# HGRN values of the 16 leading tokens: eight fp32 products in four column strips, from raw weights, for heads 2 to 7

## The reference, cut to what matters

```python
def hgrn2_mixer(q, f_pre, i_in, g, lb, norm_g):      # proj = h @ w_in_c; q, f_pre, i_in, g = split(proj, 4)
    f = lb + (1.0 - lb) * jax.nn.sigmoid(f_pre)
    log_f, k = jnp.log(f), 1.0 - f
    ...                                              # chunks of 64 tokens; the first holds 48 of padding and the 16 meta tokens
    def step(state, xs):
        qc, kc, vc, lc = xs
        b = jnp.cumsum(lc, axis=2)
        b_last = b[:, :, -1:, :]
        ...                                          # scores and the chunk's output
        state = exp(b_last)[..., None] * state + einsum('bhsd,bhse->bhde', kc * exp(b_last - b), vc)
```

## Time and profile before

| | |
|---|---|
| median of 3 runs | 1340.23 us (1338.8 to 1343.05) |
| the profiled execution | 1339.83 us |
| its span | 1337.8 us |
| granted TensorE clock, mean | 0.989 |
| PE / PEld busy | 1291.7 us (97%) / 1178.7 us (88%) |
| DVE / ACT / POOL busy | 815.8 us (61%) / 631.7 us (47%) / 323.0 us (24%) |

### The profile page before, as it was taken

The page is one execution under the profiler, slowest core; times in us unless marked ns, Lnnn a source line. Parts: engine busy times, 40 slices in busy tenths (PEclk is TensorE's granted clock), DMA queues, the critical chain, the costliest instruction groups (busy, mean ns, idle before and its releaser), DMA issues.

```text
span 1337.8 us, 23152 instructions
## 1 busy us (share of the span) xinstructions
PE 1291.7 (97%) x9766; PEld 1178.7 (88%) x9766; DVE 815.8 (61%) x1360; ACT 631.7 (47%) x982; POOL 323.0 (24%) x179
## 2 busy tenths in 40 slices
PE   7999998999999999999999999999999999999996
PEld 6999855989999999999998988877787898998984
DVE  6999654456657276384656456465557673745745
ACT  5243487445446345253465335265353462552724
POOL 0001154355110201102654124114652102011040
PEclk9999999999999999999999999999999999999997
DMA  6221100222222223223222222212212333232311
GB/s 192 89 65 33 65 1 1 68 91 64 96 95 95 95 95 99 92 95 106 84 64 64 64 64 64 64 63 95 95 64 95 95 102 100 95 114 95 106 52 63
DMA packets 109031, 108.35 MB, mean 81 GB/s; under 512 B 8096, under 2 KB 106608, under 8 KB 108928
## 3 DMA queue, kind: packets, MB, share of 16 engines
q1 hardware_dynamic: 108528, 106.77, 24.8%
q10 hardware_dynamic: 400, 0.11, 0.0%
HBM read 104.77 MB, written 2.10 MB: 80 GB/s over the span
## 4 chain that ended last, share of the span: by engine, by line
PE 80%; DVE 10%; ACT 6%; issue 2%; POOL 0%; DMA 0%; DVEq 0%; SPq 0%; ACTq 0%
PE pb L808 41%; PE pb L1014 6%; PE pb L1016 6%; PE pb L1015 6%; PE pb L977 2%; PE pb L978 2%; PE pb L979 2%; PE pb L820 1%; PE pb L1251 1%; PE pb L917 1%; PE pb L918 1%; PE pb L855 1%; PE pb L916 1%; DVE wl L2124 1%; ACT wh L1467 1%
## 5 line engine op out<-in xcount | busy, mean ns | idle before, releaser
L670 POOL TENSOR_TENSOR wl<-raw,wh 128x2048 fp32r<-128x2048 f32 x40 | 185.3, 4633 | 685.9 <-ACT wh L1467 685.9
L808 PE MATMUL pb<-hidh,wh 128*128 128x264 f32 (+1 forms) x744 | 197.9, 320 | 0.2 <-DVE wl L2124 0.2
L808 PE MATMUL pb<-hidl,wh 128*128 128x264 f32 (+1 forms) x744 | 197.5, 320 | 0.0
L808 PE MATMUL pb<-hidh,wl 128*128 128x264 f32 (+1 forms) x744 | 197.4, 320 | 0.0
L1467 ACT ACTIVATE wh<-raw 128x2048 fp32r<-128x2048 f32 x73 | 139.3, 1908 | 88.3 <-DMA raw<-in_mlp_w_down 61.0
L808 PE MATMUL pb<-hh,wh 128*128 128x264 f32 (+1 forms) x584 | 150.0, 318 | 5.0 <-DVE qd L2766 1.6
L808 PE MATMUL pb<-hh,wl 128*128 128x264 f32 (+1 forms) x584 | 145.0, 309 | 0.0
L808 PE MATMUL pb<-hl,wh 128*128 128x264 f32 (+1 forms) x584 | 144.9, 309 | 0.0
L808 PEld LDWEIGHTS pb<-hidh,wh 128*128 128x128 f32 x744 | 123.7, 188 | 10.4 <-DVE wl L2124 0.7
L808 PEld LDWEIGHTS pb<-hidh,wl 128*128 128x128 f32 x744 | 123.4, 188 | 9.7
L808 PEld LDWEIGHTS pb<-hidl,wh 128*128 128x128 f32 x744 | 123.4, 188 | 9.4
(11 more groups left out here) (472 smaller groups left out, 3260.0 us busy)
## 6 DMA issues: line engine op xcount, KB each, us to landing
raw<-in_mlp_w_up SPq DMA_DIRECT2D x32, 1024.0 KB, 5.3
raw<-in_mlp_w_down SPq DMA_DIRECT2D x32, 1024.0 KB, 5.1
raw<-in_w_in_c SPq DMA_DIRECT2D x16, 1024.0 KB, 5.3
raw<-in_w_in_ab SPq DMA_DIRECT2D x8, 1024.0 KB, 6.0
raw<-in_w_out_ab SPq DMA_DIRECT2D x4, 1024.0 KB, 5.0
raw<-in_w_out_c SPq DMA_DIRECT2D x4, 1024.0 KB, 5.1
x_tok<-in_x SPq DMA_DIRECT2D x2, 1024.0 KB, 8.0
raw<-in_s_w_glu SPq DMA_DIRECT2D x1, 1024.0 KB, 5.4
```

The source lines that it names most:

```text
L670: pool.tensor_tensor(wl[:, c % RING, :], raw[:, c % RING, :], wh[:, c % RING, :].bitcast(F32), ALU.subtract).then_inc(w_lo, 1)
L808: mm = pe.matmul(pb[:, bank + b, 0:z_ - a], lhs, rhs[:, a:z_], start=first and hi and k == 0, stop=last and k == len(todo) - 1)
```

## The change

- For p = 1 to 3 the tile of the 16 leading tokens is left out of `run_tok`. In its place `lead_values(p)` issues eight fp32 products, one for each block kc of 128 input features: 32 columns of `h` as weights (16 leading tokens and 16 others), the raw weights of the slot, 256 columns, streamed. Product kc writes to the 32 partitions from 32 (kc mod 4), so that four follow each other in four column strips of PE, and the second four are added to the first four.
- The result is not summed over the strips: each of the four groups of 32 partitions holds a part of the values. ACT copies all 128 partitions to `v1[:, 0]`. The sum over the strips comes with the product in `chunk_sums`, since the keys are laid out four times: DVE writes them to columns 0 to 15, 32 to 47, 64 to 79 and 96 to 111 of a margin of 112 in front of `kd`, zero elsewhere. The keys are turned with 112 columns instead of 16, and the product contracts over 112 rows (16 for heads 0 and 1).
- `lead_values(p)` stands in q's tile 0 after the second step (n = 1), and waits for the slot's transfer only. It uses the odd bank beside q's tile 0, which was free already.
- It reads `raw`. So POOL's low half of i{p}, which overwrites it, now also waits for `v16_done`.
- The tile k = 1 of i{p} is now the first, and still waits for q's tile 1 to be taken; k = 2 waits for q's tile 0.
- One `memset` of the margin on DVE, before layer 1.

```diff
+V16 = [STAGES[f"i{p}"][0] for p in range(1, NPAIR)]
...
+        kd_home = sb("kd", [P, 8, LEAD + L], F32, m1k)
+        kd, ke0 = kd_home[:, :, LEAD:], kd_home[:, :, 0:LEAD]
...
+            return 2 * (STAGES[f"q{p}"][2] % 2) + 1      # v16_bank(p)
...
                     pool.wait_ge(w_hi, rank(c) + 1)
+                    if c in V16:
+                        pool.wait_ge(v16_done, V16.index(c) + 1)
                     pool.tensor_tensor(wl[:, c % RING, :], raw[:, c % RING, :],
...
                     for k, (a, rows) in enumerate(starts):
+                        if c in V16 and k == 0:
+                            continue
...
+                        elif c in V16 and k == 2:
+                            pe.wait_ge(*emptied(f"q{name[1]}", 0))
...
-                pe.transpose(pb[0:16, 6, 0:P], ke[:, i % 4, 0:16], ident[:, :])
+                pe.transpose(pb[0:LEAD, 6, 0:P], ke0[:, i, :], ident[:, :])
...
-                pe.matmul(pb[:, 4, 0:P], kdt[0:16, 0, :], v1[0:16, 0, vc], start=True, stop=True, skip_group_check=True)
+                rows = 16 if i < 2 else LEAD
+                pe.matmul(pb[:, 4, 0:P], kdt[0:rows, 0, :], v1[0:rows, 0, vc], start=True, stop=True, skip_group_check=True)
...
+            def lead_values(p):
+                c = V16[p - 1]
+                pe.wait_ge(w_in[c % RING], 16 * (c // RING + 1))
+                for kc in range(KC):
+                    j = 32 * (kc % 4)
+                    mm = pe.matmul(pb[j:j + 32, v16_bank(p), 0:256], h[:, kc, 0:32], raw[:, c % RING, kc * 256:(kc + 1) * 256],
+                                   start=kc < 4, stop=kc >= 4, skip_group_check=True)
+                mm.then_inc(v16_done, 1)
...
                 def in_q(t, n):
+                    if p and t == 0 and n == 1:
+                        lead_values(p)
                     if p and t == 0 and n == 3:
                         mean_squares(a)
...
+                if p and k == 0:                          # take_v(p, k), on ACT
+                    act.wait_ge(v16_done, p)
+                    act.activation(v1[:, 0, p * 256:(p + 1) * 256], pb[:, v16_bank(p), 0:256], ACT.Copy).then_inc(emptied_by["act"], 1)
+                    return
...
+            me.step(dve.memset(ke0[:, :, :], 0.0))
...
-                TT(ke[:, n % 4, 0:NMETA], kd[:, n, 0:NMETA], elast[:, n, 0:1].broadcast_to([P, NMETA]),
-                   ALU.mult).then_inc(f_ke, 1)
+                TT(kd_home[:, n, 0:P].rearrange("p (j c) -> p j c", j=4)[:, :, 0:NMETA],
+                   kd[:, n, 0:NMETA].unsqueeze(1).broadcast_to([P, 4, NMETA]),
+                   elast[:, n, 0:1].unsqueeze(2).broadcast_to([P, 4, NMETA]), ALU.mult).then_inc(f_ke, 1)
```

More of the change, by code:

```diff
@@ L272, in trunk @@
         m1k = ExitStack()
-        kd = sb("kd", [P, 8, LEAD + L], F32, m1k)[:, :, LEAD:]
+        kd_home = sb("kd", [P, 8, LEAD + L], F32, m1k)
+        kd, ke0 = kd_home[:, :, LEAD:], kd_home[:, :, 0:LEAD]
         qd = sb("qd", [P, 8, LEAD + L], F32, m1k)[:, :, LEAD:]
@@ L481, in trunk @@
         g_prod = sem("g_prod")
+        v16_done = sem("v16_done")
         k_turned = sem("k_turned")
@@ L567, in free_bank, with v16_bank @@
             return emptied_by[by], n
+        def v16_bank(p):
+            return 2 * (STAGES[f"q{p}"][2] % 2) + 1
         def out_bank(t, half):
@@ L979, in run_tok @@
                             mm = pe.matmul(o, hl[:, kc, a:a + rows], wh[:, c % RING, w], start=False, stop=kc == KC - 1)
-                        mm.then_inc(tile_done, 1)
+                        mm.then_inc(tile_done, 2 if c in V16 and k == 1 else 1)
                         if pieces:
@@ L1974, in take_k @@
                 act.wait_ge(k_turned, i + 1)
-                act.activation(kdt[0:16, 0, :], pb[0:16, 6, 0:P], ACT.Copy).then_inc(kdt_ready, 1)
+                act.activation(kdt[0:LEAD, 0, :], pb[0:LEAD, 6, 0:P], ACT.Copy).then_inc(kdt_ready, 1)
                 act.activation(kdt[:, 1:4, :], pb[:, 4, 0:3 * P].rearrange("p (a b) -> p a b", a=3), ACT.Copy).then_inc(kdt_ready, 1)
```

## The result

| | before | after |
|---|---|---|
| median of 6 runs each | 1340.20 us | 1345.84 us |
| profiled execution | 1339.83 us | 1345.08 us |
| its span | 1337.8 us | 1343.0 us |

The changed kernel takes 1.0045 times as long (95% interval 1.0035 to 1.0056), +6.0 us (4.7 to 7.5). Either way it is slower; 24 products of 16 rows gave way to 8 strip products three times, and the time went up. The ratios leave out two executions that ran at a far lower granted clock: one of e8 (1417.32 us, 0.848) and one of the kernel before beside e1 to e4 (2111.83 us, 0.558).

What follows compares the result with a forecast made beforehand. PE, busy 97% of the span, was taken as the bound. Removing 2.74 us and adding 1.13 per pass, but with new waits, made each 1.3 longer: 1339.83 + 3.9 + 0.05 = 1343.8 us, range 1337 to 1348.5.

Steps and rivals of the forecast that it cites:

- two collisions of POOL with DVE: POOL's low halves of i2, then f3, block DVE; take_ms and q_decayed come late, each pass 1.25 us longer before restart.
- The strips: Eight fp32 strip products in q's tile 0 on PE, overlapping, add 1.13 us per pass.
- The 0.23 us of mean_squares: Behind the strips on PE, mean_squares waits less for ACT's copy, so 0.23 us per pass come back.
- the keys: Transpose with 112 columns instead of 16 on PE: between nothing and 0.11 us, eight times, mostly swallowed by waits.
- The restart behind the wait: Restarting PE's stream after its wait in front of i's first tile: 0.05 us per pass.
- the fall of the clock behind the new waits: Granted clock falling around PE's two new waits; named as a sign of being wrong, not priced.
- A: Likeliest case: POOL blocks DVE twice per pass and PE waits; 1343.8 us, own range 1342.5 to 1345.5, chance 0.62.
- E: POOL's second piece comes after q_decayed, so only keys waits, 1.1 us; 0.7 us saved per pass, 1337.7 us, chance 0.10.
- B: DVE keeps the ports past L2746, so L2752 is blocked instead; +0.8 us per pass, 1342.2 us, chance 0.10.
- C: Strips of 256 columns on PE do not overlap, 3.8 us per pass; +2.75 per pass, 1348.1 us, chance 0.06.
- D: DVE is not late for q_decayed, so PE keeps the whole 1.84 us per pass; 1334.3 us, chance 0.12.

Runs made afterwards that it cites:

- e8: Changed kernel, with POOL's low half of the slot after i also waiting until q's tile 1 is taken; -3.9 us against before, pairs -2.1.
- e1: Kernel before, with only POOL's low half of i1, i2, i3 waiting for the sixth product of q's tile 0; +6.0 us against before, pairs +5.9.
- e4: Kernel before, with only the 16 leading tokens' keys laid out four times; -1.2 us (-2.5 to +0.3) against before, pairs +0.3.
- e2: Kernel before, with only the 24 strip products added, reading the high half, result unused; +3.1 us against before, pairs +2.6.
- e9: Changed kernel, strips moved into f's tile 1, POOL's low half after i waiting until q's tile 1 is taken; -5.9 us against before, pairs -6.0.
- e6: Changed kernel, with POOL's low half of i1, i2, i3 made in four instructions of 512 columns; +3.4 us against before, pairs +2.7.

## Why the prediction was right

*The direction and the mechanism.* The likeliest case was two collisions of POOL with DVE, and it came out step by step. Put on the same clock (the scan at 776.93 instead of 774.11, so 2.82 us are added to the forecast's times), the two are:

| pair 2 | forecast | trace |
|---|---|---|
| scan over | 778.20 | 778.19 |
| POOL's low half of i2 over | 782.66 | 782.57 |
| L2746's counterpart over | 783.04 | 782.86 |
| `take_ms` over | 783.64 | 783.47 |
| PE's wait in front of `keys(b)` | 1.1 (1.2 by its own times) | 1.13 |
| f3's low half asked for | 786.87 | 786.67 |
| f3's low half over | 791.54 | 791.33 |
| `q_decayed` over | 794.03 | 793.82 |
| i2's first tile starts | 794.1 | 793.96 |

That L2746 is blocked at all stood on no row of the kernel before. It rested on the Trainium skill, "SBUF — State Buffer", section "Who interferes with whom", by which a `tensor_scalar` in a two-port mode contends with GpSimd and whoever issues first has the shared ports for the whole instruction. The counterpart's 4.76 us instead of 0.53 agree with it.

*The strips.* 1.13 us forecast; 16 records start and pass in 1.0 us, and the stream behind them is 1.2 us later (776.24 to 777.44, one spacing before the second product behind them); e2 gives 0.86 net of the 0.23 us, as forecast 0.90.

*The 0.23 us of mean_squares* came back (778.83 follows its neighbour at once), *the keys* cost 0.1 us per pair (e4).

*The sum.* 1.3 us per pair forecast, 1.03 in pairs 2 and 3 and 1.23 in pair 1 measured; 3.9 against 3.3 in all. The forecast is too high by two small terms. From the scan to the tile it had 1.25 us more than before, and 1.09 were measured, since POOL's and DVE's steps ended 0.1 to 0.2 us earlier. And the scan starts 18.78 us behind q2's high half instead of 18.90, 0.12 us that the forecast did not have. The restart behind the wait was there: from the tile's start to the next high half it is 15.58 us instead of 15.51, for which the forecast had 0.05. Missing was a term that the prediction named and left unpriced: the fall of the clock behind the new waits, 0.8 us per execution by four traces. 1343.8 us stood against medians of 1345.84 and 1344.21; the first is outside A's own range (1342.5 to 1345.5), the second inside. That the sum came so near in whole runs is in part luck: its pairs are 0.6 us too dear, and the clock and a rest that is not explained go the other way. The stated range, 1337 to 1348.5, also took in E, a faster kernel, so falling into it says less than the chain does.

*The rivals.* B (DVE keeps the ports) and C (strips apart) are out by the trace: L2746's counterpart is what is stretched, and the strips overlap. D, the kernel without lateness, did not happen, but its price was near: e9, in which neither collision reaches PE (its strips stand in f's tile 1), is 6.0 us shorter in the pairs; D had -5.5. E, one collision only, is e8: -2.1 forecast, -2.1 measured in the pairs.

## What to carry to other kernels

Before a step is given a new input to wait for, look at what its engine shares with others: the low half was not late for anybody, but 4.6 us of POOL moved onto a DVE stretch that PE waits for twice. A product that is taken out of the bound engine's stream also brings forward every wait behind it; the slack in front of the next bank (1.8 us here, less than the 2.74 us removed) is the most that can be won before something else moves. And where a change is good in its parts, the place is worth a try: the same eight products half a stage earlier, where POOL need not wait, turn +3 to +6 us into -3.4, and with one DVE step moved into -7.9.

## What the runs showed of the hardware

- DVE and POOL wait for each other not through semaphores only, as the description of the core has it, but for shared ports too. A waiting POOL instruction gets the shared ports ahead of a DVE instruction that is next in line, each time it was seen here: after the scan (777.58, with 4.76 us for L2779) and between `finish` steps (786.67, with 4.97 us for L2619). It works the other way too: in e6 DVE's waiting step goes ahead of POOL's next quarter, and the two engines take turns, with 1.26 to 1.46 us for a DVE step.
- A DVE copy of nine columns (`elast`, 0.17 us alone) took 1.26 us beside POOL's quarter in e6: small single-input copies from SBUF to SBUF are held up too. A DVE step that reads PSUM was not: L2832 took 0.69 us and `q_decayed` 0.67 beside POOL in e6, as without it.
- Behind a wait of PE of 1.6 to 1.8 us in front of i's first tile (with one of 1.1 us some 10 us earlier) the granted clock fell for a few microseconds in 2 of 12 cases of the changed kernel, at 1.5 us each, and stayed at 1.00 in the other 10. In e6, with waits of 1.8 to 2.0 us there and none earlier, it fell in 2 of 3, and behind e1's three waits of 1.8 us in front of `keys(b)` in none. What decides is not shown.
